# Gated delta rule: query products behind the prediction products, and three products written in halves of 64 columns

## What is computed

```
a_strict = einsum("bhnid,bhnjd->bhnij", k_beta, k) * decay * strict
t_inv = triangular_solve(eye + a_strict, eye)
u = t_inv @ v_beta ;  w = t_inv @ (k_beta * exp(g))
qk = einsum("bhnid,bhnjd->bhnij", q, k) * decay
def step(S, inp):                       # once per chunk, in order
    v_new = u_c - w_c @ S
    o = (q_c * exp(g_c)) @ S + qk_c @ v_new
    S = S * exp(g_last) + (k_c * exp(g_last - g_c)).T @ v_new
```

## Time and profile before

| | |
|---|---|
| Median of 3 runs | 2994.28 us |
| Lowest and highest run | 2991.57 and 3001.99 us |
| Span of the profiled execution, first to last instruction | 2990.1 us |
| Time of the profiled execution beyond its span | not recorded; the median lies 4.2 us above the span |
| TensorE busy | 2817.9 us (94%) |
| VectorE busy | 1814.3 us (61%) |
| ScalarE busy | 1181.2 us (40%) |
| GpSimd busy | 1144.1 us (38%) |
| The delta stage, first product to last | 695.4 to 1018.4 us |

### The profile page before, as it was taken

The page is one execution under the profiler, slowest core; times in us unless marked ns, Lnnn a source line. Parts: engine busy times, 40 slices in busy tenths (PEclk is TensorE's granted clock), DMA queues, the critical chain, the costliest instruction groups (busy, mean ns, idle before and its releaser), DMA issues. The chain is left out here.

```text
span 2990.1 us, 48834 instructions
## 1 busy us (share of the span) xinstructions
PE 2817.9 (94%) x18995; PEld 2440.4 (82%) x18995; DVE 1814.3 (61%) x2759; ACT 1181.2 (40%) x2210; POOL 1144.1 (38%) x1213
## 2 busy tenths in 40 slices
PE   7998979997999899998999599999999999999999
PEld 7997779996888688887788478888788888788887
DVE  3226834443555587777796677777887777543544
ACT  3226722223545365555443433333433333332321
POOL 2535930004776200001553456666666666100000
PEclk9999989997999899999999799999999999999999
DMA  8975953225454022221575633333533333654554
GB/s 269 354 251 171 263 166 111 67 74 130 108 147 87 22 75 91 85 68 40 179 246 164 216 93 105 95 103 94 190 105 99 101 105 97 240 170 146 192 167 142
DMA packets 403278, 421.07 MB, mean 141 GB/s; under 512 B 34075, under 2 KB 325995, under 8 KB 401000
## 3 DMA queue, kind: packets, MB, share of 16 engines
q1 hardware_dynamic: 368400, 298.61, 33.5%
q10 hardware_dynamic: 19944, 66.63, 6.8%
q0 software_dynamic: 14704, 52.69, 5.4%
HBM read 257.51 MB, written 160.34 MB: 140 GB/s over the span
## 5 line engine op out<-in xcount | busy, mean ns | idle before, releaser
L3526 PE MATMUL fu_pM<-fu_us_hi,fu_w_ring 128*128 128x512 f32 x2464 | 772.6, 393 | 15.2 <-DVE fu_us_lo L3361 14.3
L3526 PEld LDWEIGHTS fu_pM<-fu_us_hi,fu_w_ring 128*128 128x128 f32 x2464 | 466.3, 189 | 120.5 <-DVE fu_us_lo L3361 17.0
L3526 PE MATMUL fu_pM<-fu_us_lo,fu_w_ring 128*128 128x512 f32 x1232 | 482.8, 392 | 0.0
L3526 PEld LDWEIGHTS fu_pM<-fu_us_lo,fu_w_ring 128*128 128x128 f32 x1232 | 233.4, 189 | 47.8
L3262 ACT ACTIVATE fu_w_ring<-fu_sw 128x512 fp32r<-128x512 f32 x176 | 110.9, 631 | 325.3 <-PE fu_pM L3526 264.1
L3368 DVE TENSOR_TENSOR fu_w_ring<-fu_sw,fu_w_ring 128x512 fp32r<-128x512 f32 x132 | 139.4, 1056 | 65.4 <-ACT fu_w_ring L3262 65.3
L3368 DVE TENSOR_TENSOR fu_w_ring<-fu_w_raw,fu_w_ring 128x512 fp32r<-128x512 f32 x88 | 108.5, 1233 | 104.3 <-ACT fu_w_ring L3262 104.3
L2995 PE MATMUL fu_pM<-fu_us_hi,fu_w_ring 128*128 128x512 f32 x666 | 169.3, 391 | 1.3 <-DVE fu_w_ring L2918 1.3
L3262 ACT ACTIVATE fu_w_ring<-fu_w_raw 128x512 fp32r<-128x512 f32 x132 | 83.0, 629 | 191.3 <-PE fu_pM L3526 169.9
L3409 DVE SCALAR_TENSOR_TENSOR fu_acc<-fu_gb,fu_taps,fu_acc 128x1024 f32<-128x1024 f32 x88 | 133.0, 1513 | 37.7 <-ACT fu_acc L3303 36.9
L2075 ACT ACTIVATE at_pt_hi<-at_pT 128x512 fp32r<-128x512 f32 (+3 forms) x176 | 92.7, 539 | 143.6 <-PE at_pT L2340 142.7
(11 more groups left out here) (539 smaller groups left out, 7141.5 us busy)
## 6 DMA issues: line engine op xcount, KB each, us to landing
fu_w_ring<-scr_gs ACTq DMA_DIRECT2D x37, 704.0 KB, 4.6
fu_w_raw<-in_w_gate SPq DMA_DIRECT2D x22, 1024.0 KB, 5.4
fu_w_raw<-in_w_up SPq DMA_DIRECT2D x22, 1024.0 KB, 5.4
scr_gs<-fu_sg SPq DMA_DIRECT2D x84, 256.0 KB, 3.0
scr_gs<-fu_acc SPq DMA_DIRECT2D x63, 256.0 KB, 2.9
fu_us_lo<-scr_gs ACTq DMA_DIRECT2D x19, 704.0 KB, 4.6
pj_wd<-in_w_down POOLq DMA_DIRECT2D x11, 1024.0 KB, 9.3
scr_td<-pj_td POOLq DMA_DIRECT2D x11, 1024.0 KB, 8.0
```

The lines of the kernel that those rows point to most:

```text
L3526: p = pe.matmul(bank(2 * n + m, i)[:, :], a[:, k, :], x[:, k, :], start=(k == 0 and n_pass == 0), stop=(k == HALVES_K - 1 and n_pass == 2))
```

## The change

A part of each chunk's work is moved: Q0 and Q1 leave `outputs` and stand at the end of `predict`, right behind P0 and P1. For this each chunk has its own output tile (`pU[:, 0:2]` and `pU[:, 2:4]`, one PSUM bank), the wait for the scaled queries goes from `update(0)` to Q0, Q0 waits for `u_out` and Q1 for the copy-out of chunk 0, and VectorE's `state` waits for the new `qs` in the place of `o_done`. K is moved from behind S2 to behind P0 and Q0. The two updates and Fw are written as four products of 64x64 (`QUARTERS`) where two of 64x128 stood, and N as two products of 128x64 where one of 128x128 stood. The numbers of sums and the data are the same.

```diff
@@ -1346,6 +1346,7 @@
+        QUARTERS = ((0, 0), (1, 1), (0, 1), (1, 0))
@@ -1385,7 +1386,7 @@
-        pO, pV = pU[:, 0:2, :], pW[:, 0:2 * P].rearrange("p (g n) -> p g n", g=2)
+        pO, pV = [pU[:, 0:2, :], pU[:, 2:4, :]], pW[:, 0:2 * P].rearrange("p (g n) -> p g n", g=2)
@@ -1591,7 +1592,7 @@
-                        o = act.activation(osb[c][:, gg, :], pO[:, gg, :], ACT.Copy, scale=qscale[s][:, un:un + 1])
+                        o = act.activation(osb[c][:, gg, :], pO[c][:, gg, :], ACT.Copy, scale=qscale[s][:, un:un + 1])
@@ -1657,10 +1658,7 @@
             def state(c):
                 def run(t, s, u):
                     dve.wait_ge(ks[c], t + 1)
-                    if c == 0:
-                        dve.wait_ge(o_done[1], t)
-                    else:
-                        dve.wait_ge(o_done[0], t + 1)
+                    dve.wait_ge(qs[1 - c], t + c)
                     dve.wait_ge(s_ready[1 - c], t + c)
@@ -1685,8 +1683,8 @@
                 for un in range(UNITS):
                     c, gg = un // 2, un % 2
-                    m = pe.matmul(pB[:, UH + un:UH + un + 1], sqq[:, c, 2 * gg:2 * gg + 2, :].rearrange("p h i -> p (h i)"),
-                                  ones[:, :], start=True, stop=True)
+                    for hh, rows in enumerate(HALVES):
+                        m = pe.matmul(pB[rows, UH + un:UH + un + 1], sqq[:, c, 2 * gg + hh, :], ones[:, :], start=True, stop=True)
                 m.then_inc(qn_done[s], 1)
@@ -1751,8 +1749,9 @@
                 for un in range(UNITS):
-                    for hh, rows in enumerate(HALVES):
-                        m = pe.matmul(pS[hh][:, 2 + un // 2, un % 2 * C2:un % 2 * C2 + C2], kbg[s][rows, un, :],
+                    for hh, half in QUARTERS:
+                        rows, to = HALVES[hh], HALVES[half]
+                        m = pe.matmul(pS[hh][to, 2 + un // 2, un % 2 * C2:un % 2 * C2 + C2], kbg[s][rows, un, to],
                                       xx[s][rows, un, 1, :], start=True, stop=True)
                 m.then_inc(w_done[s], 1)
@@ -1770,17 +1769,26 @@
                     m.then_inc(ws[c], 1)
+                    if c == 0:
+                        pe.wait_ge(late_ready[s], u + 1)
+                        pe.wait_ge(u_out[s], u + 1)
+                    else:
+                        pe.wait_ge(o_out[0], t + 1)
+                    for gg in range(2):
+                        for hh, rows in enumerate(HALVES):
+                            m = pe.matmul(pO[c][rows, gg, :], qt[s][:, 2 * c + gg, hh, :], st[c][:, 2 * gg + hh, :], start=(gg == 0),
+                                          stop=False, skip_group_check=True)
+                    m.then_inc(qs[c], 1)
                 return run
 
             def update(c):
                 def run(t, s, u):
-                    if c == 0:
-                        pe.wait_ge(late_ready[s], u + 1)
                     pe.wait_ge(v_ready[c], t + 1)
                     pe.wait_ge(s_ready[1 - c], t + c)
                     for gg in range(2):
-                        for hh, rows in enumerate(HALVES):
-                            m = pe.matmul(pS[hh][:, gg, :], kd[s][rows, 2 * c + gg, :], vn[c][rows, gg, :], start=True, stop=True)
+                        for hh, half in QUARTERS:
+                            rows, to = HALVES[hh], HALVES[half]
+                            m = pe.matmul(pS[hh][to, gg, :], kd[s][rows, 2 * c + gg, to], vn[c][rows, gg, :], start=True, stop=True)
                     m.then_inc(ks[c], 1)
                 return run
@@ -1788,22 +1796,15 @@
                     if c == 0:
                         pe.wait_ge(qk_ready[s], u + 1)
-                        pe.wait_ge(o_out[1], t)
-                    else:
-                        pe.wait_ge(o_out[0], t + 1)
                     for gg in range(2):
                         for hh, rows in enumerate(HALVES):
-                            pe.matmul(pO[rows, gg, :], qt[s][:, 2 * c + gg, hh, :], st[c][:, 2 * gg + hh, :], start=(gg == 0), stop=False,
-                                      skip_group_check=True)
-                    for gg in range(2):
-                        for hh, rows in enumerate(HALVES):
-                            m = pe.matmul(pO[rows, gg, :], qk[s][rows, 2 * c + gg, :], vn[c][rows, gg, :], start=False, stop=True,
+                            m = pe.matmul(pO[c][rows, gg, :], qk[s][rows, 2 * c + gg, :], vn[c][rows, gg, :], start=False, stop=True,
                                           skip_group_check=True)
                     m.then_inc(o_done[c], 1)
                 return run
 
-            plain(DT, (0, first(1)), (-1, predict(0)), (0, second(1)), (0, first(2)), (-1, update(0)), (0, second(2)),
-                  (1, products), (0, first(3)), (-1, outputs(0)), (0, second(3)), (-1, predict(1)), (0, first(4)), (1, turn),
+            plain(DT, (0, first(1)), (-1, predict(0)), (1, products), (0, second(1)), (0, first(2)), (-1, update(0)), (0, second(2)),
+                  (0, first(3)), (-1, outputs(0)), (0, second(3)), (-1, predict(1)), (0, first(4)), (1, turn),
                   (0, second(4)), (-1, update(1)), (0, first(5)), (-1, outputs(1)), (0, second(5)), (2, q_norm), (0, final))
```

More of the change, by code:

```diff
@@ L1398, in stage_delta @@
         u_done, w_done, u_out, w_out = (r.sems(x) for x in ("u_done", "w_done", "u_out", "w_out"))
-        ws, v_ready, ks, s_ready, o_done, o_out, stored = (
-            r.sems(x) for x in ("ws", "v_ready", "ks", "s_ready", "o_done", "o_out", "stored"))
+        ws, qs, v_ready, ks, s_ready, o_done, o_out, stored = (
+            r.sems(x) for x in ("ws", "qs", "v_ready", "ks", "s_ready", "o_done", "o_out", "stored"))
         block = ctx.enter_context(nc.Block())
```

## The result

| | before | after |
|---|---|---|
| Median, 4 runs each | 2994.55 us | 2973.77 us |
| Range | 2991.57 to 3001.99 | 2967.66 to 2975.09 |
| Span of the profiled execution | 2990.1 | 2966.0 |
| Time of the profiled execution | not recorded | 2967.66 |

The ratio of the times is 0.9929, 95% interval 0.9915 to 0.9943: 21 us or 0.7% less, faster by more than the 0.3% that can be told. The forecast was 2979, range 2968 to 2997. The profiled execution after is the fastest of its four, so its span, 24 us shorter, overstates the gain a little.

The account below looks back on a forecast made before the run. TensorE's instruction list was taken as the bound almost everywhere in the turn. Fourteen turns, each 0.89 us shorter, give -12.5 us, the ends 3 more: -15.5, so a span of 2974.6 and a median of 2978.8 us; range 2968 to 2997.

Parts of the forecast that it names:

- change of shape: TensorE, between parts of different array shape: 0.15 us each, 18 per turn cut to 6, 1.8 us of array time.
- The rival of pairs: Updates and Fw: 64x64 quarters run two at a time, adding 0.44 and 0.46 us on the path; 2993 us, 12%.
- The slow feed: TensorE: records come too slowly for fours, 0.029 us each, Fw's 32 taking 0.93 us; 2986 us, 12%.
- floor of about 25 ns: TensorE: minimum start-to-start gap between matmuls however few the columns; Fw would take 0.80 us, the gain be 10.8 us.
- What lies on the path: One full turn, stretch by stretch: of 2.6 us of array time saved, 0.89 shortens the turn, 17.55 to 16.66 us.
- U0 to O0: Stretch from first update to first output: K and Q0 leave, F3 waits for VectorE; 3.95 to 2.80 us.
- Fu to P0: Stretch around Fw: Fu to Fw 0.92 us, then Fw to P0 1.36 instead of 1.87, P0 waiting for `wt`.
- T to Fu: Turn's first stretch: ScalarE's copy-out of O1 sets Fu, which starts at T + 4.72 us instead of 5.37.
- idle 0.75: TensorE's idle time in all ahead of Fu, uncovered because ScalarE's copy-out of O1 does not move; 0.75 us per turn.
- a loss of 1.13 us: P0 to U0: Q0 and K now stand ahead of the state's update, 2.72 us becoming 3.85.
- An estimated 3 more: Gain outside the fourteen full turns: first tile's turn, two without N or K, and the closing one; 3 us.
- The clock in the turns: Rival: more idle in the turn lowers TensorE's clock, 6.8 us in every turn giving 3020 us; 11%.

Follow-up runs that it names:

- shapes_only: Kernel before with only the updates, Fw and N rewritten as products of 64 columns, Q0, Q1 and K unmoved; 2966.9 us, ratio 0.9916 to before.
- n_whole: The whole change, but N as 128x128 products as before; 2973.89 us, ratio 0.9939 to before.
- k_head: As k_back, but K of tile 1 alone, in the first full turn, ahead of S1; 2962.15 us, ratio 0.9897 to before.
- k_back: The whole change, but K stays behind S2 as before; 2962.47 us, ratio 0.9898 to before.
- w_halves: The whole change, but Fw as 64x128 products as before; 2983.06 us, ratio 0.9967 to before.
- before_again: The unchanged kernel before, profiled a second time; 2993.72 us.
- pad_wait: The whole change plus 12 unread identity products between S2 and F3, where TensorE waits for VectorE; 2976.68 us, ratio 0.9948 to before.

## Why the prediction was right, point by point

- **Costs of the parts.** A change of shape at 0.15 us, N at 0.46 and the updates unchanged at 0.44 in fours hold; Fw, put at 0.46, takes about 0.5. The rival of pairs is refuted by every update after. The slow feed as it was put, 0.029 us per record, is refuted too: the last 30 records of Fw take 0.53 us, 0.018 each. The Trainium skill's floor of about 25 ns (TensorE: Matmul & The Clock Gate, Part 1) does not hold between records on different tiles.
- **What lies on the path.** 16.66 against 16.61, each stretch within 0.12. U0 to O0 was 0.12 longer than put: U0's first records now start ahead of F2's last, so the start of U0 moved and its end did not. Fu to P0 is 2.34 where 0.92 and 1.36 were put; the 1.36 holds a slip, its own terms give 1.33. T to Fu is 4.60, not 4.72, because ScalarE's copy-out ends at T + 4.51 (872.06 + 0.62 - 868.17), 0.16 sooner than put. That ScalarE sets Fu, as forecast, holds: Fu starts 0.1 us behind the copy-out in the undisturbed turns after, and N's end is not what it waits for. With nothing else to wait for, N's start to Fu is 0.56 (shapes_only), which would be T + 4.44; after, it is 0.72. The whole N (0.98) does outlast the copy-out, by 0.26 (n_whole), so of the 0.42 that the halves of N save, 0.26 is gained. What the forecast did not split is its idle 0.75: most of it lies ahead of S5, which ScalarE holds by level(5) behind causal, so that N starts at T + 3.88 where 3.35 was put, and only 0.16 lies ahead of Fu.
- **The moves.** The forecast had Q0 and K ahead of the update as a loss of 1.13 us; it is 1.03. The two halves of the change, each alone, say what that means: the rewrites give 1.6 us per turn, the moves on their own nothing, and the moves on top of the rewrites cost 0.65. Undoing K's move alone wins 0.68 back, so that the move of Q0 and Q1 is neutral. The forecast had priced the stretches rightly and not said that the change would do better without its moves.
- **The ends: the mis-sized term.** "An estimated 3 more" outside the fourteen full turns was 9.7 in the first pair of profiles and 11.3 in the second. No row of before had been laid out for it. Two causes offer themselves in the start. With K early in the first turn alone it took 39.3 us in place of 43.0 (k_head against k_back); a reason would be that tile 1 is prepared sooner. And the kernel before ran more of its start at the lower clock. Its busy time by stretch, over the second of its two falls and over 40 us of the stage's start (columns as in the earlier trace rows):

```profile
726.40:733.20 6.80, 6.80 (x88) 5.90 (x86) 1.54 (x3) 2.55 (x11) 3.40 (x8) 0.51 0.01 2
700.00:740.00 40.00, 31.04 (x520) 27.29 (x520) 11.75 (x31) 14.31 (x50) 28.52 (x43) 0.71 0.61 122
```

The kernel after, over the same 40 us:

```profile
700.00:740.00 40.00, 29.83 (x722) 26.78 (x726) 15.27 (x42) 18.17 (x63) 32.24 (x49) 0.86 0.61 126
```

The mean granted clock of these 40 us is 0.71 before and 0.86 after. None of the nine profiles with K early in the first turn has a fall between 715 and 735 us; the four with K late have one (shapes_only, k_back) or two (both profiles of before). From the first product to the third T the clock was at its lower level for 27.5 us before and 17.2 after (its mean there is 0.69 and 0.79), and for 27.6 in k_back and 19.4 in k_head. At half the pace such differences are worth at most 5.1 and 4.1 us, an estimate that would cover the whole 5.1 and 3.7. How much of it is the clock, and how much the earlier preparation, these runs cannot split: the two always came together. The end is 4.6 to 5.8 us shorter after. Its lower clock in the kernel before lasted 3.4 us of it in one profile and 5.6 in the other, by the same estimate at most 1.7 and 2.8 us. The end was 27.7 and 28.0 us long with half of the change each, without a fall, and its causes were not tried apart.
- **The clock in the turns.** The rival did not come: the holes of 0.7 us ahead of F3 left the clock at 1.00 in both profiles of the kernel after. In one other profile with the same holes (w_halves) it fell once, for 6.8 us.
- **The range.** 2973.77 lies 5 us below the forecast and 6 above the range's lower end. The forecast's median is off by the ends' 7 us less about 2 us of gaps, so that its nearness in time is in part luck; the turn's is not.

## What to carry to other kernels

Lay out one turn of the loop and ask of every part which wait ends behind it: the same 0.9 us of products costs 0.2 ahead of a wait for VectorE and its full length ahead of the state's update. Small products of one array shape next to each other saved 0.15 us per seam here, and quarters of 64x64 ran four at a time. Try the parts of a change alone: here the rewrites without the moves were no worse than both together, and with K's move undone in all turns but the first and a reordered ScalarE 1.8 times the gain was to be had.

## What the runs showed that was not expected

TensorE stops in the middle of parts, it seems because its next instructions are late. In the fourteen turns of eleven of the thirteen profiles there are places within a part, with no wait in the kernel, where over 0.45 us pass from one record's start to the next one's; before and before_again have only one of 0.3 to 0.4 us each. All 51 of them ended 1.25 to 1.7 us after a 16 KB packet of queue 8 had landed, where 7 to 9% of a stretch lies that near behind one. Both profiles of the kernel after stop ahead of the same records: the 25th of 32 of an S near 768 us, and the third of 8 of an O near 905. The time beyond fourteen undisturbed turns was 0.6 us in both profiles with turns of 17.55, 1.0 and 4.1 in the two at 16.61, 3.4 and 4.3 at 15.93, and 10.0 and 8.6 with ScalarE's new order, but only 0.9 at 15.96 in shapes_only. That each gap follows a packet is shown; that late instructions cause it is argued, and what makes the gaps more or fewer is open (pad_wait was inconclusive).
